# Gate and up weights as contiguous 2 MB units, read by a stride-four gather, in a one-core decoder layer

## What is computed

```python
logits = xt @ router_w + router_b             # 16 experts in 4 groups
# best group by the sum of its two best probabilities, then the two best experts in it
for e in range(16):
    h = silu(xt @ w_gate[e]) * (xt @ w_up[e])      # (264, 2048) @ (2048, 1024)
    y = y + combine[:, e:e+1] * (h @ w_down[e])    # (264, 1024) @ (1024, 2048)
x = layer_norm(ALPHA * x + y)
```

## Time and profile before

| | |
|---|---|
| median of 3 runs | 1800.96 us (1798.25 to 1803.58) |
| the profiled execution, its own time | 1803.73 us |
| its span, first to last instruction | 1801.9 us |
| PE busy | 1642.9 us, 91% |
| PEld (weight loads) busy | 1101.9 us, 61% |
| DVE / ACT / POOL busy | 657.4 / 383.2 / 50.6 us |
| mean granted clock of the PE | 0.969 of full speed |
| DMA traffic | 543.66 MB in 267,852 packets |

### The profile page before, as it was taken

One profiled execution on the slowest core, in us unless ns is written; L12 is line 12 of the kernel. 1 busy time (PEld: TensorE's weight loads), 2 busy tenths in 40 slices (PEclk: granted clock), 3 DMA queues, 4 the chain that ended last, 5 costly groups with the idle time before them and its releaser, 6 DMA issues.

```text
span 1801.9 us, 23350 instructions
## 1 busy us (share of the span) xinstructions
PE 1642.9 (91%) x10239; PEld 1101.9 (61%) x10239; DVE 657.4 (36%) x827; ACT 383.2 (21%) x372; POOL 50.6 (3%) x71
## 2 busy tenths in 40 slices
PE   5999999999999999985999999898898998989974
PEld 5999999988999999973343343432433434324321
DVE  5446687664357665545521020010110200102005
ACT  5453555521244333221000000000000000000001
POOL 3000000011000000002000000000000000000000
PEclk9999999997899999997999999999999999999997
DMA  9665555576555776575999999999999999999994
GB/s 256 178 176 156 145 161 148 164 194 169 146 159 144 202 238 183 151 293 219 374 424 424 423 422 425 425 425 422 425 425 424 423 425 425 426 421 425 424 425 155
DMA packets 267852, 543.66 MB, mean 302 GB/s; under 512 B 5800, under 2 KB 222904, under 8 KB 226176
## 3 DMA queue, kind: packets, MB, share of 16 engines
q1 hardware_dynamic: 264160, 529.22, 78.3%
q0 software_dynamic: 3616, 13.31, 2.5%
HBM read 535.60 MB, written 6.91 MB: 301 GB/s over the span
## 4 chain that ended last, share of the span: by engine, by line
PE 77%; DMA 16%; DVE 4%; ACT 2%; issue 1%; SPq 0%; ACTq 0%; POOL 0%; DVEq 0%
PE bank L752 15%; PE bank L497 12%; PE bank L498 12%; PE bank L499 12%; PE bank L796 11%; DMA ring_high<-wu 10%; PE bank L733 5%; PE bank L812 3%; DMA ring_low<-wd 2%; DMA ring_low<-wg 2%; PE bank L540 2%; PE bank L647 1%; DMA ring_low<-w_in 1%; PE bank L598 1%; PE bank L786 1%
## 5 line engine op out<-in xcount | busy, mean ns | idle before, releaser
L497 PE MATMUL bank<-x_hi,w_hi 128*128 128x264 f32 x1280 | 375.4, 293 | 19.4 <-DVE x_lo L1020 15.6
L498 PE MATMUL bank<-x_lo,w_hi 128*128 128x264 f32 x1280 | 370.6, 290 | 0.0
L499 PE MATMUL bank<-x_hi,w_lo 128*128 128x264 f32 x1280 | 370.0, 289 | 0.0
L1011 DVE TENSOR_TENSOR w_lo<-ring_low,w_hi 128x2048 fp32r<-128x2048 f32 x112 | 256.5, 2291 | 156.8 <-ACT w_hi L858 155.8
L497 PEld LDWEIGHTS bank<-x_hi,w_hi 128*128 128x128 f32 x1280 | 249.8, 195 | 20.8 <-issue 15.8
L752 PE MATMUL bank<-ring_high,reg_pk 128*64 128x512 f32 x1024 | 228.0, 596 | 36.3 <-DMA ring_high<-wu 33.2
L498 PEld LDWEIGHTS bank<-x_lo,w_hi 128*128 128x128 f32 x1280 | 249.9, 195 | 0.1
L499 PEld LDWEIGHTS bank<-x_hi,w_lo 128*128 128x128 f32 x1280 | 248.1, 194 | 0.0
L858 ACT CAST w_hi<-ring_low 128x2048 fp32r<-128x2048 f32 x112 | 212.8, 1900 | 140.4 <-PE bank L499 94.8
L752 PE MATMUL bank<-ring_low,reg_pk 128*64 128x512 f32 x1024 | 224.9, 593 | 11.3 <-DMA ring_low<-wg 11.3
L752 PEld LDWEIGHTS bank<-ring_high,reg_pk 128*64 128x64 f32 x1024 | 70.3, 137 | 190.1 <-issue 130.3
(11 more groups left out here) (298 smaller groups left out, 1604.2 us busy)
## 6 DMA issues: line engine op xcount, KB each, us to landing
ring_low<-w_in SPq DMA_DIRECT2D x80, 1024.0 KB, 5.8
ring_high<-wg SPq DMA_DIRECT2D x32, 2048.0 KB, 35.6
ring_low<-wu SPq DMA_DIRECT2D x32, 2048.0 KB, 24.9
ring_high<-wd SPq DMA_DIRECT2D x32, 2048.0 KB, 20.5
ring_low<-wg SPq DMA_DIRECT2D x32, 2048.0 KB, 26.3
ring_high<-wu SPq DMA_DIRECT2D x32, 2048.0 KB, 29.2
ring_low<-wd SPq DMA_DIRECT2D x32, 2048.0 KB, 33.9
ring_low<-wo SPq DMA_DIRECT2D x16, 1024.0 KB, 5.9
```

What stands on the lines that cost most here:

```text
L497: pe.matmul(out, hi[k], of_hi[:, k, :], start=(k == 0), stop=False)
L498: pe.matmul(out, hi[k], of_lo[:, k, :], start=False, stop=False)
L499: mm = pe.matmul(out, lo[k], of_hi[:, k, :], start=False, stop=(k == kk - 1))
L1011: dve.tensor_tensor(w_lo[:, q % 4, :], raw_w[:, q % 4, :], hi_of(q).bitcast(F32), ALU.subtract).then_inc(lo_ready, 1)
```

## The change

Each gate and up unit is now read with `(p k) n -> p (k n)`: partition p gets the four neighbouring rows 4p to 4p+3 of the unit's 512 (for down units the two rows 2p and 2p+1 of 256, as before). The destination is the whole slot. The gather reads x1 with a stride of four columns, 16 bytes, so that block k again holds the columns whose weight rows are in place k. Order, slots, waits and the number of matmuls and DMAs are the same.

```diff
-        x1_pairs = x1.rearrange("p a (b f w) -> p a b f w", f=P, w=2)
+        x1_fours = x1.rearrange("p a (b f w) -> p a b f w", f=P, w=4)
...
                             rows = (FF if part == 2 else D) // 4
-                            src = wt[experts[a], q * rows:(q + 1) * rows, :].rearrange("(b p k) n -> p b (k n)", p=P, k=2)
-                            sp.dma_start(ring_slot(s).rearrange("p (b c) -> p b c", b=rows // (2 * P)), src).then_inc(landed[s], 16)
+                            src = wt[experts[a], q * rows:(q + 1) * rows, :].rearrange("(p k) n -> p (k n)", p=P)
+                            sp.dma_start(ring_slot(s), src).then_inc(landed[s], 16)
...
                         k = 4 * r + j
-                        mm = pe.matmul(b[:, P * j:P * (j + 1)], x1_pairs[:, tt, k // 2, :, k % 2],
+                        mm = pe.matmul(b[:, P * j:P * (j + 1)], x1_fours[:, tt, k // 4, :, k % 4],
                                        pick[:, tt, :, :].rearrange("p a s -> p (a s)"), start=(tt == 0), stop=(tt == 2))
```

## The result

| | before | after |
|---|---|---|
| median | 1800.16 us (4 runs) | 1839.07 us (4 runs, 1837.16 to 1839.71) |
| ratio | | 1.021, 95% interval 1.0195 to 1.0225 |
| profiled execution, own time / span | 1803.73 / 1801.9 us | 1838.56 / 1836.7 us |
| PEld busy | 1101.9 us | 1192.2 us |
| packets | 267,852 | 251,468 |

What follows compares the result with a forecast made beforehand. DMA bounds the expert loop, 118.67 us a pair against TensorE's 110.07; 109 ns more per gather step makes TensorE's pair 120.53, covering the DMA saving: +26.5 us, median 1827. Whole range 1788 to 1842 us, the forecast's own 1806 to 1848.

Steps and rivals of the forecast that it cites:

- TensorE's reserve: Expert loop: TensorE has 57.2 us in hand before it, rather than DMA, sets the end.
- the saving on DMA: Expert loop's weight stream: 10.8 us saved (9.1 to 13.0), worth nothing because it lies under TensorE.
- a price of 128 ns: Extra time per gather step at which the whole range's top end, 1842 us, was cut.
- Part 1, larger pieces: Gate and up units: 0.09 us saved on each of 120; a pair's stream falls from 118.67 to 117.2 us.
- The price of stride four: Gather's weight loads: the column part doubles, adding 109 ns to each step, to some 229 ns.
- the upper end: Gather's loads: column part grows as in transposes, 2.24 times, adding 135 ns a step; last scatter +46.5 us.
- the correction left out: First gather part, already slow at reduced clock, may hide up to 2.6 us of the added load time.
- slower large pieces: Expert pairs: a pair longer than 121 us with DMA still full would mean large pieces read slower.
- Rival 1: Gather: the stride is free, only larger pieces act and DMA sets the pace; 1790 us, chance 0.27.
- Rival 2: Gather: stride costs under 75 ns, only the first gather shifts the time, -10.8 + 96 x the price; chance 0.08.
- Rival 3: Gate and up units: pieces are cut again to 8 KB and the stride is free; 1801 us, chance 0.03.

Runs made afterwards that it cites:

- experiment 1: Changed kernel with its contiguous 2 MB units but the old stride-two gather: 1791.1 us, ratio 0.9945 to before.
- experiment 2: Kernel of before, with its 8 KB pieces, but the gather reading with stride four: 1835.39 us, ratio 1.0195 to before.
- experiment 6: Changed kernel with x1 stored column-permuted in blocks of 512, so the gather reads neighbouring columns, same outputs: ratio 0.9956 to before.

## Why the prediction was right

The direction and the mechanism held: the strided load sets the gather's pace, TensorE's reserve is used up, and the saving on DMA lies under it. The size came out at +38.9 us for +26.5, 12 us above the forecast of 1827. That the stated range held (1839.07, its top end 1842 being meant for a price of 128 ns) is in part luck: the price measured gives 29.3 us as worked out below, about 1830, and the rest is a term that the range did not hold.

- **Part 1, larger pieces.** Right, at the low end: a pair's stream fell by 1.21 us, not 1.44, and the units alone gave 10 us, not 10.8 (experiment 1). That two 8 KB packets cost more than one of 16 KB could be read from the down units that already had them.
- **The price of stride four.** 235.5 - 120 = 115.5 ns for my 109, close by two errors that went against each other. The column part of the load did not double, it grew from 109 to 242 ns, 2.2 times, which is the factor of the transposes that I had kept for the upper end; so the load got 133 ns longer. And I had let the step take over all of that, where it took 115.5 ns (at stride three 57 of 65, at stride eight 121 of 140).
- **The cover that is gone.** The reserve of 57.2 us was used up as computed. From the first gather step to the last scatter the two profiles take 939.1 and 977.9 us, 38.8 us apart. The terms: the first gather part +0.6 (it was already at 224 ns a step at the low clock, so it hid 2.2 us of the at most 2.6 that the correction left out allowed); three more parts, 5.81 - 3.04 each, +8.3; the gather for pair 1, +11.1; six more, +66.5; less the reserve, 57.2. That is 29.3 us, against 26.5.
- **The term I missed.** The rest, 9.5 us, is nearly all the clock: it falls more often on work that nothing covers. In pair 0 the second down product takes 15.68 us instead of 13.98 (the first paid this in both kernels), and one down product does so in five of the next six pairs (122.5 to 122.7 us against 120.95 in the one without). Six times 1.7 is 10.2 us; pieces a little faster than in the earlier trace rows (27.47 for 27.64 us of gate and up) give 1.4 back, and the last pair adds 0.7, the one landing that TensorE still waits for. Before had four falls too, but the first is that of both kernels, and the other three (1222.97, 1697.42 and 1752.03 us) lie under waits for units. I had taken every piece but the gather at its old duration.
- **DMA saving worth nothing.** Right: experiment 2 is no slower than the changed kernel.
- **Signs named beforehand.** Loads of 300 ns or more: 329. Ninety-six steps in 20 to 24 us: 22.61. 16,384 packets fewer: exactly. Scatters 120 to 121 us apart: 122.66, the clock again. That is longer than the 121 us that I named as a sign of slower large pieces, but DMA was not full in that pair (24 units in 122.66 us are 410 GB/s), and the units alone need 117.46 us for them.
- **Rivals.** Rival 1 (a free stride) is what experiments 1 and 6 make true by other means; their times, 1789.3 to 1791.5 and 1789.2 to 1794.2 us, stand against the 1790 that I had priced. Rival 2 is not this kernel's case, but its rule held for stride three. Rival 3 is out by the packet count.

The profiled execution moved by 34.8 us and the medians by 38.9, because its stages before the experts happened to be 3.9 us shorter (first gather step at 828.22 us, not 832.16).

## What to carry to other kernels

A faster transfer is worth no more than the reserve of the next engine, and it pays nothing if the layout that buys it makes that engine slower: count both bounds for one period before trading. In a matmul of this shape a float32 stationary operand was read at a stride of two for 4 ns (in the transposes of the earlier trace rows the same stride cost 67 ns a load); from there each further 16-byte line costs, so put a permutation into a copy that has time (here the evacuation of PSUM and a product off the path) rather than into the matmul's read. And when a stretch of multiplies slows down, price the clock of what follows it too.

## What the runs showed of the hardware, unexpected

- A gather's weight load of 128 float32 columns costs 87 ns and 1.7 to 1.95 ns for every 16-byte line it touches, from 64 lines up (1.69 and 1.89 ns in transposes with 32 and 64 lines); stride eight (336 ns) is hardly worse than stride four (329 ns).
- TensorE's clock fell to half for 3.4 us at a time: six or seven times in the expert stage with gather steps of 235 to 241 ns, two to four times with steps of 114 to 177 ns. Each fall beside ordinary multiplies cost 1.7 us, beside load-bound ones 0.16 us (5.96 for 5.80).
- ScalarE writing SBUF every 16 bytes took 7.65 us for 4096 columns instead of 3.62; VectorE reading PSUM every 16 bytes took 674 ns instead of 676.
